# A two-layer hybrid encoder block on one core: the last third of the four mixers in another order on TensorE, VectorE and ScalarE

## The chip, the core and the metric

The kernel runs on one core of one Trainium2 chip. The metric is the device time of one execution in microseconds (us); lower is better. Beside the time of whole runs there is one profiled execution, and all rows below are of that one.

## What is computed

The block has two layers (DEPTH = 2) over 256 tokens of width 1024, in float32. Each layer normalises the input, projects it once into nine slices of 256 columns, sends the slices through four mixers of width 256 each, normalises each mixer's output by itself, joins the four, multiplies by `w_out`, scales by the gate `g1` and adds to the input. Then comes a feed-forward part: dense SwiGLU in layer 0, top-2-of-8 experts in layer 1.

```python
for l in range(DEPTH):
    mod = c_act @ w_mod[l] + b_mod[l]
    sh1, sc1, g1, sh2, sc2, g2 = jnp.split(mod, 6, axis=-1)
    h = modulate(rms_norm(x, norm_mix[l]), sh1, sc1)
    proj = h @ w_in[l]
    pa, pu, pv, px, pg, dq, dfz, di, dg = jnp.split(proj, N_IN_SLICES, axis=-1)
    ya = rms_norm(pool_mixer(pa, pool_w[l], pool_scale[l]), pool_out_norm[l])
    yb = rms_norm(sgu_mixer(pu, pv, sgu_ws[l], sgu_b[l]), sgu_out_norm[l])
    yc = rms_norm(lru_mixer(px, pg, ...), lru_out_norm[l])
    yd = hgrn_mixer(dq, dfz, di, dg, lower_bounds[l], hgrn_out_norm[l])
    y = jnp.concatenate([ya, yb, yc, yd], axis=-1) @ w_out[l]
    x = x + g1[:, None, :] * y
    h = modulate(rms_norm(x, norm_ffn[l]), sh2, sc2)
    f = swiglu(...) if l % 2 == 0 else moe_ffn(...)
    x = x + g2[:, None, :] * f
```

Mixer a is a causal pooling (a banded matrix over time, then a 64x64 product per head), b a causal spatial gating inside blocks of 128 tokens, c a gated linear recurrence, d a gated recurrence with a 64x64 state per head that is carried over chunks of 16 tokens.

## The kernel before, in words

The program is written engine by engine: TensorE, VectorE, ScalarE, GpSimd and the sync engine each have one list of instructions in a fixed order, and semaphores join them. `STEPS` names the steps that an engine marks ("mix_t" for TensorE's steps in the mixers, "mix_v" for VectorE's, "mix_a" for ScalarE's); another engine waits with `wait_ge(mix_t.sem, mix_t.at(name, l))`. VectorE and ScalarE wait for each of their own instructions to end before the next. So the order in these lists is the order of the work.

Weights come through a ring of six slots of 2 MB each; the sync engine issues their loads in the order of `chunks` and issues a load when the user of the slot's last content is done (L528). In layer 0 the order is: modulation parts sh1, sc1, the five chunks of `w_in`, then sh2, sc2, g1, g2 (two halves each), two halves of `w_out`, then the feed-forward chunks. So the first feed-forward chunk waits for the first half of g1 to be summed, the second for the second half of g1, the next two for the halves of g2.

The modulation vectors of layer 0 are summed on VectorE between the mixers' steps: `mod_part(0, n)` multiplies each 128x512 block of two chunks by a column and adds it into `mod_acc[:, n % 2]` (L1172, L1174; eight instructions to a half, n = 3 is sc2, 4 is g1, 5 is g2). TensorE then sums over the partitions: `row_sum_columns` (L687, sixteen recorded matmuls with one column) for sh and sc, `row_sum_wide` (L707, two 128x512 matmuls) for the gates. `gate` on VectorE adds the bias (L1206).

The last third of the mixers starts where TensorE ends `scores(1)` (L799: matmuls with two moving columns, for mixer d). All bank numbers below are PSUM banks.

- TensorE, in order: d's full part from the scores (L816, bank 3), d's part from the states, 60 matmuls of 64x64 by 16 columns (L823, bank 3, step "o"), b's bias and gating (L834, L839, bank 4, step "z"), in layer 0 the column sum of sc2, then the sum of squares of d over heads (L850, "ssd"), of c ("ssc", `channel_sum`, L754), a's banded product (L861, L863, "aband"), the sum of squares of b ("ssb"), a's block product (L873, "apool"), `row_sum_wide` for g1, the sum of squares of a ("ssa"). Then the output projection (L892): 32 matmuls of 128x512, each recorded as two, in four groups of eight, in the order of mixers c, d, b, a; each group waits for its mixer's normalised output ("yc1", "yd1", "yb1", "ya1"). Banks 0 to 3 hold the result.
- ScalarE: squares and square roots around these, each named sq or rt with the mixer's letter; "gu" (Gelu of pu), "pa", "pd", "ps0", "ps1" copy and scale.
- VectorE: "sf0", "sf1", b's mean and variance to "vn1", in layer 0 `mod_part(0, 4)` (both halves of g1) and the columns of sc2, "yb_raw", then for d, c, b, a in this order the reciprocal of the root (L1397 for d, 128x512; L1407 for the others, 128x256), and two scaled products to `y_t` (L1401, L1410).

After the mixers VectorE runs `gate` for g1, in layer 0 then `mod_part(0, 5)` (both halves of g2) and three subtractions that prepare the first feed-forward weights (L1436), and then the residual: for each of four banks a product (L1235) and a sum (L1237). The norm of the next part follows, and the feed-forward part begins on TensorE (L921).

Of the kernel before, what the change touches and what calls it, by code (L numbers as in the profile page):

```python
# [101 lines left out]
class Steps:  # L102
# [11 lines left out]
    def said(self, name):  # L114
# [13 lines left out]

STEPS = {
# [100 lines left out]
def hybrid_stream_block(nc, a, out):  # L230

    ctx = ExitStack()
    with ctx:
# [136 lines left out]
        def mark(ins, s, name):  # L370

            s.said(name)
# [63 lines left out]
        def mod_bank(l, n):  # L436

            return bank[7] if l == 0 and n >= 2 else bank[n] if l == 0 else bank[0]
# [233 lines left out]
        def _(eng):  # L672
# [53 lines left out]
            def mixers(l):  # L726
# [83 lines left out]
                scores(1)  # L810
                eng.wait_ge(mix_v.sem, mix_v.at("wst", l))
# [7 lines left out]
                eng.wait_ge(mix_v.sem, mix_v.at("qt", l))  # L819
                for h in range(NH):  # L820
# [6 lines left out]
                mark(ins.then_inc(mix_t.sem, 1), mix_t, "o")  # L827

                eng.wait_ge(mix_v.sem, mix_v.at("vn1", l))
                eng.wait_ge(mix_v.sem, mix_v.at("wst", l))  # L830
# [12 lines left out]
                if l == 0:  # L843
                    row_sum_columns(0, "sc2")

                eng.wait_ge(mix_a.sem, mix_a.at("sqd", l))
                eng.wait_ge(chain_v.sem, chain_v.at("s", l * CHAIN + CHAIN - 1))
                if l == 0:
                    eng.wait_ge(mod_e.sem, mod_e.at("fin", 3))
                mark(mm(bank[7][:, :], head_ones, tmp[:, 2, :], start=True, stop=True).then_inc(mix_t.sem, 1),  # L850
                     mix_t, "ssd")
                eng.wait_ge(mix_a.sem, mix_a.at("sqc", l))
                eng.wait_ge(mix_a.sem, mix_a.at("i1", l))
                channel_sum(bank[5], tmp[:, 8, :], "ssc")

                eng.wait_ge(mix_a.sem, mix_a.at("pa", l))
                eng.wait_ge(mix_v.sem, mix_v.at("sf1", l))
                eng.wait_ge(s_const, N_CONSTS)
                for g in range(NH):
                    q, i = g % 2, g // 2  # L860
                    mm(bank[6][q * HD:(q + 1) * HD, i * T:i * T + EDGE], tmp[:, 11, g * HD:(g + 1) * HD],  # L861
                       band_a[:, g, :], start=i == 0, stop=False, skip_group_check=True)
                    ins = mm(bank[6][q * HD:(q + 1) * HD, i * T + P:(i + 1) * T],  # L863
                             tmp[:, 11, G + g * HD:G + (g + 1) * HD], band_b[:, g, :],
                             start=False, stop=True, skip_group_check=True)
                mark(ins.then_inc(mix_t.sem, 1), mix_t, "aband")
                eng.wait_ge(mix_a.sem, mix_a.at("sqb", l))
                eng.wait_ge(mix_a.sem, mix_a.at("rtd", l))
                channel_sum(bank[7], tmp[:, 4, :], "ssb")
                eng.wait_ge(mix_a.sem, mix_a.at("pd", l))  # L870
                eng.wait_ge(mix_v.sem, mix_v.at("yb_raw", l))
                for i in range(CB):
                    ins = mm(bank[4][:, i * T:(i + 1) * T], blocks[:, 0, i, :], tmp[:, 6, i * T:(i + 1) * T],  # L873
                             start=True, stop=True)
                mark(ins.then_inc(mix_t.sem, 1), mix_t, "apool")
                eng.wait_ge(mix_a.sem, mix_a.at("rtb", l))
                row_sum_wide(l, 0, (bank[6], bank[7]))
                eng.wait_ge(mix_a.sem, mix_a.at("sqa", l))
                eng.wait_ge(mix_a.sem, mix_a.at("rtc", l))
                channel_sum(bank[5], tmp[:, 1, :], "ssa")  # L880
# [3 lines left out]
                for name in ("gate_d", "gu", "pa"):  # L884
                    eng.wait_ge(mix_a.sem, mix_a.at(name, l))
                eng.wait_ge(mix_v.sem, mix_v.at("od", l))
                for n, (name, g) in enumerate((("yc1", 2), ("yd1", 3), ("yb1", 1), ("ya1", 0))):
                    eng.wait_ge(mix_v.sem, mix_v.at(name, l))
                    for tt in range(TT):
                        for half in range(2):  # L890
                            for i in range(2 * g, 2 * g + 2):
                                ins = mm(bank[2 * tt + half][:, :], y_t[:, i, tt * P:(tt + 1) * P],  # L892
# [255 lines left out]
        def _(eng):  # L1148
            tt_, ts_, stt = nc.vector.tensor_tensor, nc.vector.tensor_scalar, nc.vector.scalar_tensor_tensor

            def mod_part(l, n):
# [8 lines left out]
                for half in range(2):  # L1160
# [79 lines left out]
            def mixers(l):  # L1240
                def v(ins, name):
                    done(eng, ins, mix_v, name, l)
# [146 lines left out]
                if l == 0:  # L1389
                    mod_part(0, 4)  # L1390
                    mod_columns(0, "sc2")
                eng.wait_ge(mix_t.sem, mix_t.at("z", l))
# [10 lines left out]
                for n, (name, at, rt, src, par_name) in enumerate((("c", 4, 9, 12, "lru_out"), ("b", 2, 10, 7, "sgu_out"),  # L1403
                                                              ("a", 0, 2, 3, "pool_out"))):
                    eng.wait_ge(mix_a.sem, mix_a.at(f"rt{name}", l))
                    r = t(rt)[:, 0:T]
                    v(nc.vector.reciprocal(r, r).then_inc(mix_v.sem, 1), f"rec_{name}")  # L1407
                    for i in range(CB):
                        c = slice(i * T, (i + 1) * T)
                        v(stt(out=y_t[:, at + i, :], in0=t(src)[:, c], scalar=par(par_name, l, i), in1=r,  # L1410
                              op0=ALU.mult, op1=ALU.mult).then_inc(mix_v.sem, 1), f"y{name}{i}")
# [282 lines left out]
            for l in range(DEPTH):  # L1694
# [4 lines left out]
                gate(l, 0, (bank[6], bank[7]))  # L1699
# [4 lines left out]
                residual(2 * l, [bank[n][:, :] for n in range(4)], [[(mix_t, f"wout{n}", l)] for n in range(4)])  # L1704
# [22 lines left out]
        def _(eng):  # L1727
# [27 lines left out]
            def mixers(l):  # L1755
# [64 lines left out]
                s(act(t(8), t(12), ACT.Square).then_inc(mix_a.sem, 1), "sqc")  # L1820
                eng.wait_ge(mix_v.sem, mix_v.at("vc1", l))
                for tt in range(TT):
# [5 lines left out]
                eng.wait_ge(mix_t.sem, mix_t.at("pu", l))  # L1828
                s(act(t(7), bank[1][:, :], ACT.Gelu_apprx_tanh).then_inc(mix_a.sem, 1), "gu")
                eng.wait_ge(mix_t.sem, mix_t.at("pa", l))  # L1830
                s(act(t(11), bank[2][:, :], ACT.Copy).then_inc(mix_a.sem, 1), "pa")
# [5 lines left out]
                eng.wait_ge(mix_t.sem, mix_t.at("ssc", l))  # L1837
                s(act(t(9)[:, 0:T], bank[5][:, 0:T], ACT.Sqrt, bias=eps_col[:, 0:1], scale=1.0 / G).then_inc(mix_a.sem, 1),
                  "rtc")
                eng.wait_ge(mix_t.sem, mix_t.at("aband", l))  # L1840
                s(act(t(6), bank[6][:, :], ACT.Copy).then_inc(mix_a.sem, 1), "pd")
                eng.wait_ge(mix_v.sem, mix_v.at("yb_raw", l))
                s(act(t(4), t(7), ACT.Square).then_inc(mix_a.sem, 1), "sqb")
                eng.wait_ge(mix_t.sem, mix_t.at("ssb", l))
                s(act(t(10)[:, 0:T], bank[7][:, 0:T], ACT.Sqrt, bias=eps_col[:, 0:1], scale=1.0 / G).then_inc(mix_a.sem, 1),
                  "rtb")
                eng.wait_ge(mix_t.sem, mix_t.at("apool", l))
                for i in range(CB):
                    c = slice(i * T, (i + 1) * T)
                    s(act(t(3)[:, c], bank[4][:, c], ACT.Copy, scale=par("pool_scale", l, i)).then_inc(mix_a.sem, 1),  # L1850
                      f"ps{i}")
                s(act(t(1), t(3), ACT.Square).then_inc(mix_a.sem, 1), "sqa")
                eng.wait_ge(mix_t.sem, mix_t.at("ssa", l))
                eng.wait_ge(mix_v.sem, mix_v.at("od", l))
                eng.wait_ge(mix_v.sem, mix_v.at("yd1", l))
                s(act(t(2)[:, 0:T], bank[5][:, 0:T], ACT.Sqrt, bias=eps_col[:, 0:1], scale=1.0 / G).then_inc(mix_a.sem, 1),
                  "rta")
# [229 lines left out]
```

## Time and profile before

| | |
|---|---|
| median of three runs | 1695.45 us (1695.25 to 1698.53) |
| the profiled execution | 1696.81 us |
| its span, first to last instruction | 1695.1 us |
| mean granted TensorE clock | 0.958 of full speed |
| busy: TensorE matmul, weight load | 95%, 79% |
| busy: VectorE, ScalarE | 78%, 58% |
| one of 40 slices of the page | 42.4 us |

The busy shares are averages over very different stages. The experts take the time from about 655 us to 1690 us, the dense feed-forward part that from 218 us to 470 us, and the two passes through the mixers' last third, which are what the change touches, lie from 145 us to 210 us and from 573 us to 633 us. The granted clock takes two values, 1.00 (2.4 GHz) and 0.50 (1.2 GHz); values between are stretches that hold both.

### The profile page before, as it was taken

To read this page: it belongs to the slowest core of one execution; us is meant where nothing else is said; L and a number is where in the kernel's file an instruction comes from. 1 tells how busy PE (TensorE), PEld (TensorE's weight loads), DVE (VectorE), ACT (ScalarE), POOL (GpSimd) and SP (SyncE) were. 2 spreads that over 40 slices of the span, in tenths; PEclk is the share of its full clock that TensorE was granted. 3 is DMA by queue.
4 is the path that set the end of the run, shared out by engine and by line. 5 is a ranking of instruction groups with operands and counts; after the bars stand their busy time and mean duration, and the time that the engine had idled before them with its cause. 6 is when DMAs were issued, how large, how long until landed. Compare 5 with 4: busy or idle time off the path is not lost.

```text
span 1695.1 us, 19855 instructions
## 1 busy us (share of the span) xinstructions
PE 1610.8 (95%) x8005; PEld 1332.3 (79%) x8005; DVE 1327.2 (78%) x1266; ACT 987.2 (58%) x895; POOL 38.8 (2%) x108
## 2 busy tenths in 40 slices
PE   5999889999979997999999999999999999999994
PEld 5699489999867846888888888888888888888883
DVE  5687868878666255878978978988988988988985
ACT  1442244433352325777777777777777777777772
POOL 5100000000000000000000000000000000000000
PEclk9986999999998797999999999999999999999997
DMA  9648456888832204989999999999999989999970
GB/s 354 217 149 301 166 203 248 299 309 314 295 112 100 100 25 157 367 329 368 351 329 367 349 331 362 352 334 356 357 335 350 362 332 350 360 333 351 370 269 39
DMA packets 157000, 481.07 MB, mean 284 GB/s; under 512 B 4202, under 2 KB 6422, under 8 KB 156902
## 3 DMA queue, kind: packets, MB, share of 16 engines
q1 hardware_dynamic: 154976, 475.02, 76.0%
q0 software_dynamic: 1392, 3.58, 0.7%
q8 instruction: 65, 1.06, 0.3%
q10 hardware_dynamic: 534, 1.13, 0.2%
q14 instruction: 33, 0.27, 0.0%
HBM read 478.66 MB, written 1.05 MB: 283 GB/s over the span
## 4 chain that ended last, share of the span: by engine, by line
issue 63%; PE 29%; DVE 4%; ACT 1%; DMA 1%; POOL 1%; SPq 1%; DVEq 0%; ACTq 0%; POOLq 0%
PE bank L747 4%; PE bank L892 3%; PE bank L921 3%; PE bank L922 3%; PE bank L923 3%; PE bank L799 2%; PE bank L744 2%; PE bank L936 2%; PE bank L937 2%; PE bank L938 2%; PE bank L823 1%; DMA ring<-in_w_mod_dram 1%; PE bank L687 1%; PE bank L779 1%; DVE tri L1296 1%
## 5 line engine op out<-in xcount | busy, mean ns | idle before, releaser
L1549 DVE TENSOR_TENSOR ring_low<-ring,w_high 128x2048 fp32r<-128x2048 f32 x336 | 766.8, 2292 | 128.0 <-ACT w_high L1919 121.5
L1919 ACT ACTIVATE w_high<-ring 128x2048 fp32r<-128x2048 f32 x336 | 643.8, 1919 | 243.5 <-PE bank L995 241.7
L993 PE MATMUL bank<-w_high,x_high 128*128 128x512 f32 x896 | 358.1, 400 | 1.1 <-DVE x_low L1525 1.1
L994 PE MATMUL bank<-ring_low,x_high 128*128 128x512 f32 x896 | 352.9, 394 | 0.0
L995 PE MATMUL bank<-w_high,x_low 128*128 128x512 f32 x896 | 350.0, 391 | 0.0
L995 PEld LDWEIGHTS bank<-w_high,x_low 128*128 128x128 f32 x896 | 168.4, 188 | 41.0
L993 PEld LDWEIGHTS bank<-w_high,x_high 128*128 128x128 f32 x896 | 168.5, 188 | 39.6 <-DVE ring_low L1549 1.5
L994 PEld LDWEIGHTS bank<-ring_low,x_high 128*128 128x128 f32 x896 | 167.9, 187 | 34.9
L993 PE MATMUL bank<-w_high,act_high 128*128 128x512 f32 x448 | 179.9, 402 | 3.6 <-DVE ring_low L1549 3.6
L995 PE MATMUL bank<-w_high,act_low 128*128 128x512 f32 x448 | 177.0, 395 | 0.0
L994 PE MATMUL bank<-ring_low,act_high 128*128 128x512 f32 x448 | 175.9, 393 | 0.0
L1864 ACT ACTIVATE tmp_r<-ring 128x1024 fp32r<-128x1024 f32 x84 | 88.9, 1061 | 146.4 <-PE bank L923 86.5
L1436 DVE TENSOR_TENSOR ring_low<-ring,tmp_r 128x1024 fp32r<-128x1024 f32 x84 | 102.2, 1225 | 45.5 <-ACT tmp_r L1864 43.1
L921 PE MATMUL bank<-h_high,tmp_r 128*128 128x256 f32 x448 | 128.1, 286 | 4.6 <-DVE h_low L1443 4.6
L922 PE MATMUL bank<-h_high,ring_low 128*128 128x256 f32 x448 | 127.2, 284 | 0.0
L923 PE MATMUL bank<-h_low,tmp_r 128*128 128x256 f32 x448 | 126.2, 282 | 0.0
L993 PEld LDWEIGHTS bank<-w_high,act_high 128*128 128x128 f32 x448 | 84.2, 188 | 28.9 <-DVE ring_low L1549 8.4
L995 PEld LDWEIGHTS bank<-w_high,act_low 128*128 128x128 f32 x448 | 84.0, 187 | 20.4
L994 PEld LDWEIGHTS bank<-ring_low,act_high 128*128 128x128 f32 x448 | 84.4, 188 | 18.6
L747 PE MATMUL bank<-h_t,ring 128*128 128x256 f32 x384 | 90.7, 397 | 2.3 <-POOL band_a L638 2.0
L921 PEld LDWEIGHTS bank<-h_high,tmp_r 128*128 128x128 f32 x448 | 85.8, 191 | 5.3 <-issue 5.0
L747 PEld LDWEIGHTS bank<-h_t,ring 128*128 128x128 f32 x384 | 76.2, 200 | 15.2 <-issue 2.2
(305 smaller groups left out, 1801.4 us busy)
## 6 DMA issues: line engine op xcount, KB each, us to landing
ring<-in_moe_w_dram SPq DMA_DIRECT2D x168, 2048.0 KB, 7.9
ring<-in_w_mod_dram SPq DMA_DIRECT2D x23, 2048.0 KB, 11.0
ring<-in_ffn_w_dram SPq DMA_DIRECT2D x21, 2048.0 KB, 12.0
ring<-in_w_in_dram SPq DMA_DIRECT2D x8, 2048.0 KB, 15.1
ring<-in_w_out_dram SPq DMA_DIRECT2D x4, 2048.0 KB, 14.3
ring<-in_w_mod_dram SPq DMA_DIRECT2D x2, 1024.0 KB, 15.9
ring<-in_w_in_dram SPq DMA_DIRECT2D x2, 1024.0 KB, 18.6
gate_row<-in_b_mod_dram POOLq DMA_DIRECT2D x4, 512.0 KB, 7.3
```

The source lines that it names most:

```text
L747: ins = mm(b[:, i * T:(i + 1) * T], w[:, k, off + i * P:off + (i + 1) * P], h_t[:, k, :], start=k == 0, stop=k == KB - 1)
L892: ins = mm(bank[2 * tt + half][:, :], y_t[:, i, tt * P:(tt + 1) * P], wide(("wout", l, half))[:, i, :], start=n == 0 and i == 2 * g, stop= ...
L921: mm(o, w_h[:, k, :], h_high[:, k, :], start=k == 0, stop=False)
L922: mm(o, w_l[:, k, :], h_high[:, k, :], start=False, stop=False)
L923: ins = mm(o, w_h[:, k, :], h_low[:, k, :], start=False, stop=k == KB - 1)
L993: mm(out_, x_h, w_h, start=first, stop=False)
L994: mm(out_, x_h, w_l, start=False, stop=False)
L995: return mm(out_, x_l, w_h, start=False, stop=last)
L1436: mark(tt_(quarter(ring_low, QUARTERS[m]), quarter(ring, QUARTERS[m]), quarter_high(m).bitcast(F32), ALU.subtract).then_inc(ffn_l.sem, 1), ...
L1549: tt_(moe_low(u, m // 2)[:, c], moe_slot(u, m // 2)[:, c], w_high[:, m % HIGHS, :].bitcast(F32), ALU.subtract).then_inc(low_made, 1)
L1864: mark(act(quarter_high(m), quarter(ring, QUARTERS[m]), ACT.Copy).then_inc(ffn_h.sem, 1), ffn_h, "q")
L1919: act(w_high[:, m % HIGHS, :], moe_slot(u, m // 2)[:, c], ACT.Copy).then_inc(high_made, 1)
```

## The change

The same operations are done in both layers; their order and some buffers and banks change.

- TensorE: after `scores(1)` come, in this order, in layer 0 the column sum of sc2 (now in bank 5), "ssc" (bank 0), "aband" (bank 7), d's full part, then the 60 state matmuls of d in four parts of 15 (`from_states(h)`), with "apool" (bank 6) after the first, "z" after the second, and "ssa" (bank 1) after the third. After the fourth ("o") come "ssb" (bank 2), "ssd" (bank 7) and the output projection, whose groups run in the order c, a, b, d and whose banks are 0, 1, 2 and 4.
- `row_sum_wide` for g1 moves from ahead of the projection into it, ahead of the fourth group (banks 5 and 6).
- ScalarE: "gu" and "pa" move up behind "sqc"; then "rtc", "pd", the squares and root of b's variance, "ps0", "ps1", "sqa", "rta", "sqb", "rtb", "sqd", "rtd".
- VectorE: the order of the mixers is c, a, then "yb_raw", b, d. In layer 0 the columns of sc2 come ahead of all that, the first half of g1 is summed between c and a, and the second half behind d. `gate`, `mod_part(0, 5)`, the three subtractions and the residual follow as before.

```diff
+WOUT_BANKS = (0, 1, 2, 4)
...
     "mix_v":
...
-         "cv10 cv11 cv12 xc1 qt a2 m m0 ix bb hs0 hs1 yc_raw sf0 sf1 mu vc0 vc1 rvr vn0 vn1 yb_raw rec_d "
-         "od yd0 yd1 rec_c yc0 yc1 rec_b yb0 yb1 rec_a ya0 ya1").split(),
+         "cv10 cv11 cv12 xc1 qt a2 m m0 ix bb hs0 hs1 yc_raw sf0 sf1 mu vc0 vc1 rvr vn0 vn1 rec_c "
+         "yc0 yc1 rec_a ya0 ya1 yb_raw rec_b yb0 yb1 rec_d od yd0 yd1").split(),
     "mix_a":
...
-        ("sig lna lnb lnk eb ea kh q kt xp gate_c gv0 gv1 r0 r1 i0 i1 a0 a1 th0 th1 sm gate_d sqc sv0 sv1 "
-         "rv gu pa sqd rtd rtc pd sqb rtb ps0 ps1 sqa rta").split(),
+        ("sig lna lnb lnk eb ea kh q kt xp gate_c gv0 gv1 r0 r1 i0 i1 a0 a1 th0 th1 sm gate_d sqc gu pa rtc pd "
+         "sv0 sv1 rv ps0 ps1 sqa rta sqb rtb sqd rtd").split(),
     "mix_t":
...
-        ("dfz ws di dq kt px u0 u1 u2 u3 u4 u5 u6 u7 pg pv wa wx sc0 dg pu pa sc1 o z ssd ssc aband ssb "
-         "apool ssa wout0 wout1 wout2 wout3").split(),
+        ("dfz ws di dq kt px u0 u1 u2 u3 u4 u5 u6 u7 pg pv wa wx sc0 dg pu pa sc1 ssc aband apool z ssa "
+         "o ssb ssd wout0 wout1 wout2 wout3").split(),
...
@@ TensorE, behind scores(1)
+                if l == 0:
+                    eng.wait_ge(mix_a.sem, mix_a.at("i1", l))
+                    row_sum_columns(0, "sc2")
...
+                channel_sum(bank[0], tmp[:, 8, :], "ssc")
...
+                def from_states(h):
...
+                eng.wait_ge(mix_v.sem, mix_v.at("qt", l))
+                from_states(0)
...
+                from_states(1)
...
+                from_states(2)
...
+                channel_sum(bank[1], tmp[:, 1, :], "ssa")
+                mark(from_states(3).then_inc(mix_t.sem, 1), mix_t, "o")
+                eng.wait_ge(mix_a.sem, mix_a.at("sqb", l))
+                channel_sum(bank[2], tmp[:, 4, :], "ssb")
                 eng.wait_ge(mix_a.sem, mix_a.at("sqd", l))
...
-                eng.wait_ge(mix_a.sem, mix_a.at("rtb", l))
-                row_sum_wide(l, 0, (bank[6], bank[7]))
...
-                for n, (name, g) in enumerate((("yc1", 2), ("yd1", 3), ("yb1", 1), ("ya1", 0))):
+                eng.wait_ge(mix_v.sem, mix_v.at("yb_raw", l))
+                for n, (name, g) in enumerate((("yc1", 2), ("ya1", 0), ("yb1", 1), ("yd1", 3))):
+                    if n == 3:
+                        eng.wait_ge(mix_a.sem, mix_a.at("ps1", l))
+                        if l == 0:
+                            eng.wait_ge(mod_e.sem, mod_e.at("fin", 3))
+                        row_sum_wide(l, 0, (bank[5], bank[6]))
                     eng.wait_ge(mix_v.sem, mix_v.at(name, l))
...
@@ VectorE, behind vn1
                 if l == 0:
-                    mod_part(0, 4)
                     mod_columns(0, "sc2")
...
+                scaled("c", 4, t(9)[:, 0:T], 12, "lru_out")
+                if l == 0:
+                    mod_part(0, 4, (0,))
+                scaled("a", 0, t(10)[:, T:2 * T], 8, "pool_out")
                 eng.wait_ge(mix_t.sem, mix_t.at("z", l))
                 eng.wait_ge(mix_a.sem, mix_a.at("gu", l))
                 v(tt_(t(7), t(7), bank[4][:, :], ALU.mult).then_inc(mix_v.sem, 1), "yb_raw")
+                scaled("b", 2, t(10)[:, 0:T], 7, "sgu_out")
...
+                if l == 0:
+                    mod_part(0, 4, (1,))
...
-                gate(l, 0, (bank[6], bank[7]))
+                gate(l, 0, (bank[5], bank[6]))
                 if l == 0:
                     mod_part(0, 5)
                     for m in range(HIGHS):
                         quarter_rest(m)
```

## Rows read from the trace of the kernel before

**Rows 1.** The page, section 2: the granted TensorE clock in 40 slices.

```profile
PEclk9986999999998797999999999999999999999997
```

**Rows 2.** Timeline of layer 0, VectorE: start us, us, engine, line.

```profile
185.95 1.42 DVE L1206 TENSOR_TENSOR gate_row<-bank,gate_row 128x512 f32<-128x512 f32 x2
...
193.96 5.48 DVE L1174 SCALAR_TENSOR_TENSOR mod_acc<-ring,c_act,mod_acc 128x512 f32<-128x512 f32 x7
...
199.47 3.50 DVE L1436 TENSOR_TENSOR ring_low<-ring,tmp_r 128x1024 fp32r<-128x1024 f32 x3
...
202.99 0.69 DVE L1235 TENSOR_TENSOR h_t<-bank,gate_row 128x512 f32<-128x512 f32 x1
...
208.94 0.69 DVE L1237 TENSOR_TENSOR x<-x,h_t 128x512 f32<-128x512 f32 x1
```

**Rows 3.** Timeline of layer 0, TensorE: scores, states, sums, projection.

```profile
134.80 10.61 PE L799 MATMUL bank<-head_sel,tri 128*128 128x2 f32 x64
...
146.38 1.97 PE L816 MATMUL bank<-v_wide,tmp 128*64 128x128 f32 x16 [0.97 <-DVE v_wide L1372]
...
148.28 11.78 PE L823 MATMUL bank<-tmp,state 64*64 64x16 f32 x120
...
163.90 3.58 PE L687 MATMUL bank<-consts,mod_acc 128*128 128x1 f32 x16
...
180.40 27.70 PE L892 MATMUL bank<-ring,xn 128*128 128x512 f32 x64 [0.89 <-DVE xn L1410]
```

**Rows 4.** Timeline of layer 0, the single operations that change places.

```profile
169.93 1.91 PE L754 MATMUL bank<-tmp,consts 128*128 128x256 f32 x4
...
170.22 1.28 ACT L1835 ACT_TABLE_LOAD   x1 [9.46 <-PE bank L850]
...
172.31 3.35 DVE L1397 RECIPROCAL tmp<-tmp 128x512 f32<-128x512 f32 x1 [3.63 <-ACT tmp L1835]
...
173.92 0.63 ACT L1843 ACTIVATE tmp<-tmp 128x512 f32<-128x512 f32 x1
...
174.60 1.13 PE L754 MATMUL bank<-tmp,consts 128*128 128x256 f32 x4 [1.41 <-ACT tmp L1843]
...
175.83 0.47 ACT L1845 ACTIVATE tmp<-bank,eps_col 128x256 f32<-128x256 f32 x1 [1.28 <-PE bank L754]
...
176.43 1.91 PE L707 MATMUL bank<-mod_acc,consts 128*128 128x512 f32 x4
176.69 0.98 ACT L1850 ACTIVATE tmp<-bank,params 128x256 f32<-128x256 f32 x2 [0.39 <-PE bank L873]
...
177.46 1.75 DVE L1407 RECIPROCAL tmp<-tmp 128x256 f32<-128x256 f32 x1
...
179.25 1.01 DVE L1410 SCALAR_TENSOR_TENSOR xn<-tmp,params 128x256 f32<-128x256 f32 x2
```

**Rows 5.** Windows of TensorE: length, busy (matmul records), granted clock, DMA share, GB/s.

```profile
100.20:103.90 3.70, 3.70 (x35) 1.00 0.95 359
104.00:110.00 6.00, 6.00 (x30) 0.50 0.30 112
110.30:114.00 3.70, 3.70 (x10) 0.50 0.00 0
```

**Rows 6.** Timeline of layer 1: TensorE and VectorE.

```profile
563.45 9.32 PE L799 MATMUL bank<-head_sel,tri 128*128 128x2 f32 x64
...
603.60 27.70 PE L892 MATMUL bank<-ring,xn 128*128 128x512 f32 x64 [0.86 <-DVE xn L1410]
...
632.14 0.69 DVE L1237 TENSOR_TENSOR x<-x,h_t 128x512 f32<-128x512 f32 x1
```

**Rows 7.** Windows of all engines: PE, PEld, DVE, ACT, POOL, clock, DMA.

```profile
152.00:156.00 4.00, 4.00 (x44) 4.00 (x44) 3.82 (x6) 1.19 (x2) 0.00 (x0) 0.50 1.05 386
...
218.00:470.00 252.00, 248.12 (x1748) 232.35 (x1748) 189.42 (x215) 101.75 (x104) 0.00 (x0) 0.99 0.76 275
```

**Rows 8.** Timeline of layer 0, the sync engine's loads of feed-forward weights.

```profile
157.87 41.96 SPq L528 DMA_DIRECT2D ring<-in_ffn_w_dram  x4
```

More of the change, by code:

```diff
@@ L436, in mod_bank @@
         def mod_bank(l, n):
-            return bank[7] if l == 0 and n >= 2 else bank[n] if l == 0 else bank[0]
+            return bank[(0, 1, 7, 5)[n]] if l == 0 else bank[0]
         def slot(n):
@@ L854, in mixers @@
[L854 to L874, printed above, removed]
@@ L875, in mixers @@
-                mark(ins.then_inc(mix_t.sem, 1), mix_t, "apool")
-                eng.wait_ge(mix_a.sem, mix_a.at("rtb", l))
-                row_sum_wide(l, 0, (bank[6], bank[7]))
-                eng.wait_ge(mix_a.sem, mix_a.at("sqa", l))
-                eng.wait_ge(mix_a.sem, mix_a.at("rtc", l))
-                channel_sum(bank[5], tmp[:, 1, :], "ssa")
                 for half in range(2):
                     arrived(eng, ("wout", l, half))
-                for name in ("gate_d", "gu", "pa"):
+                for name in ("rtc", "rta", "rtb"):
@@ L891, in mixers @@
                             for i in range(2 * g, 2 * g + 2):
-                                ins = mm(bank[2 * tt + half][:, :], y_t[:, i, tt * P:(tt + 1) * P],
+                                ins = mm(bank[WOUT_BANKS[2 * tt + half]][:, :], y_t[:, i, tt * P:(tt + 1) * P],
                                          wide(("wout", l, half))[:, i, :], start=n == 0 and i == 2 * g,
@@ L1159, in mod_part @@
                     eng.wait_ge(gate_t.sem, gate_t.at("sum", 2 * (l - 1) + n))
-                for half in range(2):
+                for half in halves:
                     key = ("mod", l, MOD_PARTS[n], half)
@@ L1402, in mixers @@
                           op0=ALU.mult, op1=ALU.mult).then_inc(mix_v.sem, 1), f"yd{i}")
[L1403 to L1411, printed above, removed]
+                if l == 0:
+                    mod_part(0, 4, (1,))
             def mod_step(n, step):
@@ L1703, in _ @@
                         quarter_rest(m)
-                residual(2 * l, [bank[n][:, :] for n in range(4)], [[(mix_t, f"wout{n}", l)] for n in range(4)])
+                residual(2 * l, [bank[n][:, :] for n in WOUT_BANKS], [[(mix_t, f"wout{n}", l)] for n in range(4)])
                 norm_x(2 * l + 1)
@@ L1827, in mixers @@
                   "rv")
[L1828 to L1831, printed above, removed]
+                eng.wait_ge(mix_t.sem, mix_t.at("apool", l))
+                for i in range(CB):
+                    c = slice(i * T, (i + 1) * T)
+                    s(act(t(8)[:, c], bank[6][:, c], ACT.Copy, scale=par("pool_scale", l, i)).then_inc(mix_a.sem, 1),
+                      f"ps{i}")
+                s(act(t(1), t(8), ACT.Square).then_inc(mix_a.sem, 1), "sqa")
+                eng.wait_ge(mix_t.sem, mix_t.at("ssa", l))
+                s(act(t(10)[:, T:2 * T], bank[1][:, 0:T], ACT.Sqrt, bias=eps_col[:, 0:1], scale=1.0 / G).then_inc(mix_a.sem, 1),
+                  "rta")
+                eng.wait_ge(mix_v.sem, mix_v.at("yb_raw", l))
+                s(act(t(4), t(7), ACT.Square).then_inc(mix_a.sem, 1), "sqb")
+                eng.wait_ge(mix_t.sem, mix_t.at("ssb", l))
+                s(act(t(10)[:, 0:T], bank[2][:, 0:T], ACT.Sqrt, bias=eps_col[:, 0:1], scale=1.0 / G).then_inc(mix_a.sem, 1),
+                  "rtb")
                 eng.wait_ge(mix_t.sem, mix_t.at("o", l))
@@ L1836, in mixers @@
                   "rtd")
[L1837 to L1857, printed above, removed]
             def quarter_first(m):
@@ L2044, in _ @@
                 if l == 0:
[L2045 removed]
+                    eng.wait_ge(mix_v.sem, mix_v.at("yd1", l))
                     for m in range(HIGHS):
```

52 lines of the change are left out of this document (38 added, 14 removed).

## The prediction

> **What bounds the kernel now.** I read the page's clock line first, then timelines of both mixer tails with all engines, then windows for the clock, last the sync engine's loads. The clock line shows full speed nearly everywhere with dips where the mixers run [rows 1]. In the tail of layer 0 TensorE is the path: scores, states, norm sums, then the projection without a break from 180.40 for 27.70 us, eight matmuls in 27.70/4 = 6.93 us [rows 3]. Behind the last mixer's output VectorE has a row of its own that is as long: gate at 185.95 (1.42), g2's two halves from there to 193.96 + 5.48 = 199.44 (12.04, so 6.0 a half), three subtractions to 202.97, and at 202.99 the residual [rows 2]. From the start of the gate to the residual that is 17.04 us with no idle time. TensorE's first result bank is done at 180.40 + 20.8 + 1.7 = 202.9. So both engines arrive together, with no slack on either. The residual ends at 209.63 [rows 2]. In layer 1 g2 is summed elsewhere, VectorE waits for TensorE, and the residual ends at 632.83 [rows 6].
>
> **The pieces, at both clocks.** TensorE's clock falls in the scores although it is never idle there: 35 records in 3.70 us at 1.00, 30 in 6.00 at 0.50 [rows 5]. So loads of weights also take twice as long at half clock. A norm sum (two 128x256 matmuls) takes 1.85 at half clock before the next matmul starts (1.91 to its end) and 0.87 at full, being 1.13 with its drain [rows 4]; until ScalarE starts I take 2.1 and 1.25. apool has the same shape. The full part takes 1.9 at half, aband with 1088 columns for 1024 takes 2.0. The states take 11.78 at half clock, 2.93 a quarter [rows 3, 7], and by the ratio of the scores 1.47 at full. From the states' end (160.06) to the sc2 sum (163.90) z takes 3.9 at half, 2.0 at full; the sc2 sum 3.5 to the next matmul [rows 3]. ScalarE: square 0.65, root 0.47, the two scalings 0.98. A mixer's three VectorE steps take 1.75 + 1.01 = 2.8 with the gap; d's end needs 3.35 first [rows 4]. yb_raw reads and writes 128x512 once, as a residual product does: 0.7 [rows 2].
>
> **Edit 1, the reordering up to the projection.** Two schedules bound it. In H the clock stays at 0.50 until the projection. In F it comes back once ssc, aband and the full part (5.75 us of dense matmuls) are through, holds over the states, and is lost again where TensorE runs dry before ssb.
>
> Layer 0, H, from the scores' end at 145.4: sc2 sum 148.95, ssc 150.8, aband 152.8, full part 154.7, states 157.6, apool 159.3, states 162.3, z 166.2, states 169.1, ssa 171.0, rta 171.7. Now a chain over three engines: a on VectorE 174.6, yb_raw 175.3, sqb 176.05, ssb for ScalarE 178.2, rtb and sqd 179.35, ssd 181.2. The projection starts at 181.2, against 180.40. F is equal to 154.7, then 156.2, 157.0, 158.5, 160.5, 162.0, 162.85, rta 163.5. Here VectorE is late: g1's first half runs from 159.4 to 165.4. So a 168.2, yb_raw 168.9, sqb 169.7, ssb (half clock again, as TensorE was idle for 5 us) 171.8, rtb and sqd 172.95, ssd 174.85: the projection starts at 174.85.
>
> Layer 1 begins at 563.45 + 9.32 = 572.8 [rows 6]. H by the same steps: full part 578.6, rta 595.6, sqb 600.0, ssd 605.15. F: full part 578.6, ssa 586.75, rta 587.35, sqb 591.7, ssd 596.85, against 603.60 before. To F I add 1.0 us for small gaps at changes of matmul form, which the sums of lengths leave out; layer 0 hides it behind VectorE.
>
> The new waits sit on ScalarE: behind sqb wait rtb, sqd, rtd, all of them needed. b's variance now stands behind rtc and pd, ends at about 155 and gives vn1 at 156.2, while z starts after 158.5: hidden by 2 us. The function table load ahead of rtd, 1.28 us [rows 4], leaves the path; new loads ahead of gu and rtc are hidden by the scores and by the same 2 us.
>
> **Edit 2, the projection.** Groups c, a, b are ready at its start or 3 us after, d some 6 us after ssd (0.7 + 3.35 + 0.7 + 1.01); d is needed 20.8 us on. All hidden. `row_sum_wide` was in a gap of the old norm chain; it now adds its two 128x512 matmuls, 1.73 us, to both projections. At the start the clock is low in both schedules. After scores(0) dense work ran at 0.50 for 4 us [rows 5]; ssd is 1.85 of them, the other 2.1 cost half, 1.1 us (bounds 0 and 1.8).
>
> **Edit 3, what waits for the gate.** This is the large term. `gate` needs `row_sum_wide`, which now stands behind three groups, and g2's sums, the subtractions and the residual stand behind `gate` on VectorE. g1's second half ends near 187 (F) or 194 (H) and VectorE then idles. With the projection starting at S: three groups 20.8, clock 1.1, wide sum 1.73 and 0.17 to VectorE, then the 17.04 us above, then the residual of 4 x 1.45 = 5.8. The residual ends at S + 46.6. Before it ended at S + 29.2. Layer 0: F 221.5, that is +11.9; H 227.8, +18.2. In layer 1 VectorE has no g2 sum and TensorE sets the end: S + 1.1 + 1.73 + the 29.2 of before, so F 597.85 + 32.0 = 629.9, -3.0 against 632.83 (gaps included), and H 637.2, +4.3.
>
> What makes this certain is that TensorE's matmuls run in the order of its list. The Trainium skill says so in "TensorE: Matmul & The Clock Gate", section "Step-by-step: what each phase is for": only weight loads are pulled ahead of running matmuls, the matmuls stay in program order. The trace agrees, each group of rows 3 starts after the one ahead of it; could the wide sum pass the first groups, it would run when g1 is done and layer 0 would lose some 9 us less.
>
> **Loads.** SP's queue is moved too. The first feed-forward chunk was issued at 157.87 when g1's first half was summed [rows 8]; it goes at about 165.4, the second at about 187 to 194, g2's two behind the late sums at about 206 to 219. ScalarE needs the second for its third preparation, ahead of the residual at 215; it has over 15 us. The others are needed in the ninth step or later of a part that begins after 229. Nothing, but if the second came 15 us late it would add directly.
>
> **The sum.** F: +11.9 - 3.0 = +8.9. H: +18.2 + 4.3 = +22.5. F in one layer alone: +16.2 or +15.3. All behind moves along one for one: in the dense part TensorE is busy 248.12 of 252 us at 0.99 clock [rows 7], so its start sets its end. I take F, since the one stretch of rows 5 where dense work followed scores came back in 4 us and here 5.75 are dense. The profiled execution took 1696.81, its span 1695.1 and 1.7 outside; the median is 1695.45. F gives 1705.7 for the profiled and 1704.4 for the median.
>
> **Rivals.** (1) H, or H in one layer: the dense stretch before the states does not bring the clock back, or the states lose it again. For it: the scores lost it while TensorE was busy, and it stays at half all through the states [rows 7]. 1711 to 1718. (2) The clock stays up to the end of the projection. By the skill's same page, section "What's actually happening", the clock follows how busy the engine has been lately; TensorE is never idle from the scores to the end of the states, and read so it would be full early and stay. Worked out from rows: ssb and ssd at full save 1.85, the projection 1.1, in each layer: +8.9 - 5.9 = +3, 1698.5. Rows 5 speak against busy alone being enough. (3) The other side, not slower: the lost time is absorbed. If the dense part waited for weights, a later start would cost nothing from the point where the ring is 12 us behind; layer 0 would be neutral and layer 1's -3.0 would be left, 1692.5. Rows 7 speak against it: DMA at 0.76 and TensorE idle under 4 us. (4) The norm tail's chain in layer 0 is longer than I took (VectorE later than 165.4): up to +3 on F.
>
> **Chances.** F 0.50, with (4) 0.10 inside; one layer H 0.22, both H 0.13, (2) 0.10, (3) 0.02, the rest 0.03 near no change. The range leaves out (3) and most of both H: 1698 to 1716. A change of 0.2%, 3.4 us, is about what a measurement of this kernel tells from none. Faster 0.03, same 0.07, slower 0.90.
>
> **What would show it.** In the profile after: in layer 0 an idle stretch of VectorE of over 8 us that ends at `gate` on TensorE's wide sum; the residual starting 17 us behind it and long after the last projection matmul; TensorE idle for some 20 us between projection and next norm. In layer 1 a projection of 29.5 us or more with the wide sum inside and no such gap. Clock windows between 155 and 165 tell F (1.00) from H (0.50). I am wrong if `gate` runs before the projection's third group ends, or if the dense part is shorter than before.

## The result and the profile after

The changed kernel takes 1709.8 us (median of four runs, 1709.19 to 1710.39) against 1696.09 us before: a ratio of 1.0078, 95% interval 1.0061 to 1.0096. The prediction was 1704.4 with a range of 1698 to 1716 and 0.90 on slower. The profiled execution has a span of 1707.4 us against 1695.1.

To compare the two traces I count from the end of `scores(1)`, where the changed part begins, to the start of the output projection and from there to the end of the residual. F and H are the two schedules of the prediction: in F the full clock comes back for the states, in H it stays at half up to the projection.

| us | before | after | F | H |
|---|---|---|---|---|
| layer 0: scores' end to projection | 35.0 | 31.5 | 29.5 | 35.8 |
| layer 0: projection to residual's end | 29.2 | 47.4 | 46.6 | 46.6 |
| layer 0, sum | 64.2 | 78.9 | 76.1 | 82.4 |
| layer 1: scores' end to projection | 30.8 | 28.0 | 25.1 | 32.4 |
| layer 1: projection to residual's end | 29.2 | 31.9 | 32.0 | 32.0 |
| layer 1, sum | 60.1 | 59.9 | 57.1 | 64.4 |

So the changed parts are 14.7 us longer in layer 0 and 0.1 us shorter in layer 1. These are the parts of one profile; further passes follow with the experiments. The spans differ by only 12.3 because this execution came to the end of layer 0's scores 3.7 us sooner, and lost 1.5 us elsewhere; none of that code is touched (the last section tells why such differences occur).

The timeline of VectorE in layer 0, after. The rows answer to [rows 2]; the bracket is the idle time ahead of a row and what ended it.

```profile
179.96 5.48 DVE L1186 SCALAR_TENSOR_TENSOR mod_acc<-ring,c_act,mod_acc 128x512 f32<-128x512 f32 x7
...
197.91 1.42 DVE L1218 TENSOR_TENSOR gate_row<-bank,gate_row 128x512 f32<-128x512 f32 x2 [12.47 <-PE bank L710]
...
199.89 5.48 DVE L1186 SCALAR_TENSOR_TENSOR mod_acc<-ring,c_act,mod_acc 128x512 f32<-128x512 f32 x7
...
205.92 5.48 DVE L1186 SCALAR_TENSOR_TENSOR mod_acc<-ring,c_act,mod_acc 128x512 f32<-128x512 f32 x7
211.43 3.50 DVE L1455 TENSOR_TENSOR ring_low<-ring,tmp_r 128x1024 fp32r<-128x1024 f32 x3
...
214.85 0.68 DVE L1247 TENSOR_TENSOR h_t<-bank,gate_row 128x512 f32<-128x512 f32 x1
...
219.92 0.69 DVE L1249 TENSOR_TENSOR x<-x,h_t 128x512 f32<-128x512 f32 x1
```

g1's second half is summed at 185.44, and then VectorE stands idle for 12.47 us until the wide sum (now L710) is there. Gate, g2's sum, the subtractions and the residual follow without a break, from 197.91 to 220.61. The timeline of TensorE, after, answers to [rows 3]:

```profile
132.07 9.65 PE L802 MATMUL bank<-head_sel,tri 128*128 128x2 f32 x64
...
153.37 1.92 PE L848 MATMUL bank<-tmp,state 64*64 64x16 f32 x30
...
157.65 3.38 PE L848 MATMUL bank<-tmp,state 64*64 64x16 f32 x30
...
168.00 2.07 PE L757 MATMUL bank<-tmp,consts 128*128 128x256 f32 x4 [1.66 <-ACT tmp L1866]
...
171.33 2.07 PE L886 MATMUL bank<-tmp,consts 128*128 128x512 f32 x2 [1.25 <-ACT tmp L1871]
...
173.19 22.87 PE L904 MATMUL bank<-ring,xn 128*128 128x512 f32 x48
...
195.90 1.88 PE L710 MATMUL bank<-mod_acc,consts 128*128 128x512 f32 x4
...
197.61 7.03 PE L904 MATMUL bank<-ring,xn 128*128 128x512 f32 x16
...
221.65 3.68 PE L719 MATMUL bank<-consts,xn 128*128 128x128 f32 x16 [17.00 <-DVE xn L1226]
```

The wide sum stands at 195.90, behind three groups of the projection. The projection is done at 204.64, which is 62.9 us behind the scores' end (62.7 before), and then TensorE waits 17.00 us for a norm that VectorE brings late. The chain of work that ended last, in order of time, runs over the same points:

```profile
179.75 16.31 PE bank L904 x38
196.06 1.73 PE bank L710 x4
197.91 0.70 DVE gate_row L1218
...
211.43 3.50 DVE ring_low L1455 x3
...
220.84 0.76 DVE xn L1226
```

In layer 1 VectorE also waits for the wide sum, 17.48 us, but has no g2 to sum behind it, and the residual keeps up with TensorE. Timelines of both engines, answering to [rows 6]:

```profile
612.16 21.84 PE L904 MATMUL bank<-ring,xn 128*128 128x512 f32 x48
...
633.84 1.88 PE L710 MATMUL bank<-mod_acc,consts 128*128 128x512 f32 x4
...
635.56 7.03 PE L904 MATMUL bank<-ring,xn 128*128 128x512 f32 x16
635.86 1.42 DVE L1218 TENSOR_TENSOR gate_row<-bank,gate_row 128x512 f32<-128x512 f32 x2 [17.48 <-PE bank L710]
...
643.42 0.69 DVE L1249 TENSOR_TENSOR x<-x,h_t 128x512 f32<-128x512 f32 x1
```

The clock in layer 0, windows of all engines, after (the clock is the third number from the right), answering to [rows 7]:

```profile
144.00:149.50 5.50, 5.50 (x33) 4.67 (x34) 0.25 (x1) 2.05 (x3) 0.00 (x0) 0.50 1.05 387
151.00:156.00 5.00, 5.00 (x65) 4.56 (x64) 4.36 (x9) 1.79 (x4) 0.00 (x0) 1.00 1.05 387
157.50:162.00 4.50, 4.50 (x36) 4.13 (x34) 3.89 (x6) 0.00 (x0) 0.00 (x0) 0.50 0.85 309
...
173.00:177.00 4.00, 4.00 (x6) 1.69 (x5) 3.22 (x3) 0.69 (x1) 0.00 (x0) 0.50 0.00 2
178.00:195.00 17.00, 17.00 (x41) 7.47 (x40) 7.09 (x11) 3.06 (x3) 0.00 (x0) 1.00 0.36 124
```

It was back at 150, as F has it, and gone again at 157, ahead of the third quarter of the states, while TensorE was busy without a gap. The second quarter took 1.92 us, the third 3.38. In the kernel before the clock stood at half from the scores through the states, but it was back at 172.3, 8 us ahead of the projection, and that projection ran at full clock from its start. Windows of TensorE, before (the clock is again the third number from the right):

```profile
171.50:172.00 0.50, 0.50 (x3) 0.50 1.03 381
172.50:173.00 0.50, 0.50 (x12) 1.00 1.05 389
```

### The profile page after: what moved, and what is told of

Its sections match the earlier page's. It is cut to its first block, busy times and chain, and to the rows that moved or that the text cites. A ratio compares the mean times of both kernels' runs of the same rounds, so it can differ in the third digit from the quotient of the medians.

```text
span 1707.4 us, 19844 instructions
## 1 busy us (share of the span) xinstructions
PE 1609.9 (94%) x8005; PEld 1327.9 (78%) x8005; DVE 1328.4 (78%) x1266; ACT 985.0 (58%) x893; POOL 38.8 (2%) x108
## 4 chain that ended last, share of the span: by engine, by line
issue 62%; PE 30%; DVE 4%; DMA 1%; ACT 1%; POOL 0%; SPq 0%; DVEq 0%; ACTq 0%; POOLq 0%
PE bank L750 4%; PE bank L933 3%; PE bank L934 3%; PE bank L935 3%; PE bank L904 3%; PE bank L802 2%; PE bank L747 2%; PE bank L948 2%; PE bank L949 2%; PE bank L950 1%; DMA ring<-in_w_mod_dram 1%; PE bank L690 1%; PE bank L848 1%; PE bank L757 1%; PE bank L782 1%
## 5 line engine op out<-in xcount | busy, mean ns | idle before, releaser
L1455 DVE TENSOR_TENSOR ring_low<-ring,tmp_r 128x1024 fp32r<-128x1024 f32 x84 | 102.2, 1225 | 46.6 <-ACT tmp_r L1881 44.2
```

Source lines behind the costliest of these rows:

```text
L1455: mark(tt_(quarter(ring_low, QUARTERS[m]), quarter(ring, QUARTERS[m]), quarter_high(m).bitcast(F32), ALU.subtract).then_inc(ffn_l.sem, 1), ...
```

## The experiments

Four kernels (g2's sum ahead of gate, the wide sum one group earlier, the new order in layer 1 alone, the wide sum in the gaps) ran on one chip with 32 runs of the kernel before (median 1696.64), the other four on another chip with 11 (median 1695.91). The ratios are to the kernel before on the same chip. They are estimates with an interval and not quotients of two medians, from which they differ by up to 0.2%, so both are given where it matters. "The two parts" are, for one profiled execution, the times of the table above.

**g2's sum ahead of gate.** Edit of the changed kernel, on VectorE in layer 0:

```diff
-                gate(l, 0, (bank[5], bank[6]))
                 if l == 0:
                     mod_part(0, 5)
+                gate(l, 0, (bank[5], bank[6]))
+                if l == 0:
                     for m in range(HIGHS):
                         quarter_rest(m)
```

> The changed kernel with one edit on VectorE in layer 0: the sum of g2 (12.0 us) goes ahead of gate instead of behind it. Theory: the loss is the chain wide sum, gate, g2, subtractions, residual. The 12.5 us that VectorE idled ahead of gate then hold g2's sum; gate, the subtractions and the residual follow the wide sum at once, so the residual starts some 12 us earlier (202.9 instead of 214.85 on the changed kernel's clock) and the kernel takes 1709.8 - 12 = 1698. Rival, the norm chain or the wide sum inside the projection is the loss: no more than 2 us come back. Rival, the dense part's weights come late: no change.

Measured: 1702.88 us, ratio 1.0031 (1.0017 to 1.0045). In the profile the two parts of layer 0 are 31.5 + 35.3 = 66.7 us, 12.1 less than in the changed kernel. Timeline of VectorE of this kernel:

```profile
191.55 5.48 DVE L1186 SCALAR_TENSOR_TENSOR mod_acc<-ring,c_act,mod_acc 128x512 f32<-128x512 f32 x7
197.35 1.42 DVE L1218 TENSOR_TENSOR gate_row<-bank,gate_row 128x512 f32<-128x512 f32 x2 [0.32 <-PE bank L710]
198.80 3.50 DVE L1455 TENSOR_TENSOR ring_low<-ring,tmp_r 128x1024 fp32r<-128x1024 f32 x3
202.22 0.68 DVE L1247 TENSOR_TENSOR h_t<-bank,gate_row 128x512 f32<-128x512 f32 x1
```

The idle 12.47 us ahead of gate are 0.32 now. The trace shows the 12 us. Whole runs show 7 by the medians (1709.8 to 1702.88) and 8 by the ratios (1.0078 to 1.0031 is 0.47%), where 12 and 1698 were expected. This profile lost 5.5 us against the changed kernel's in a stretch of layer 1 that no edit touches (the last section). That most of the other runs lost it there too is not shown. The theory holds for the chain; the size in whole runs came out smaller than expected.

**The wide sum one group earlier.** Edit on TensorE:

```diff
-                    if n == 3:
+                    if n == 2:
                         eng.wait_ge(mix_a.sem, mix_a.at("ps1", l))
```

> The changed kernel with one edit on TensorE: the wide sum of g1 stands ahead of the third group of the projection instead of the fourth. Theory: g1 is summed at 185.4, the third group would begin at about 189, so the wide sum ends 6.9 us (one group of eight matmuls) earlier in layer 0, and gate, g2's sum and the residual with it; layer 1 keeps its time, since there TensorE sets the end and the projection is as long. 1709.8 - 6.9 = 1703. Rival, VectorE's order alone matters and not the wide sum's place: no change. Rival, the length of the projection is the loss: no change.

Measured: 1708.49 us, ratio 1.0050 (1.0033 to 1.0067), single runs from 1703.54 to 1710.3. In layer 0 the part behind the projection's start is 39.6 us, 7.8 less than 47.4: one group (6.93) and 0.9 because this projection lost less to half clock. Timelines of VectorE and TensorE:

```profile
194.59 1.88 PE L710 MATMUL bank<-mod_acc,consts 128*128 128x512 f32 x4
```

```profile
196.60 1.42 DVE L1218 TENSOR_TENSOR gate_row<-bank,gate_row 128x512 f32<-128x512 f32 x2 [4.67 <-PE bank L710]
```

gate starts 16.9 us behind the projection's start (179.69) instead of 24.7, and the residual's end moves with it. The place of the wide sum in TensorE's list counts, not VectorE's order alone. In this execution the projection itself began 2.8 us later than in the changed kernel's profile, counted from the scores' end. The whole did not reach the forecast of 1703: it gained 1.3 us by the medians and 4.7 by the ratios, whose intervals just overlap. So this experiment stands on its trace, not on its whole runs.

**The new order in one layer alone.** Both kernels hold both orders of the three engines' `mixers` and of the step lists and take one for each layer:

```diff
+            def mixers(l):
+                (mixers_old, mixers_new)[l](l)      # layer1_only; the other: (mixers_new, mixers_old)
```

> Layer 0 in the old order, layer 1 in the new one. The changed kernel's trace has the loss in layer 0 (+14.8 us from the end of the scores to the end of the residual) and -0.1 in layer 1. Theory: 1696 within 1 us, the same as before. My F schedule said -3.0 for layer 1 and H +4.3; 1693 or 1700 would say that layer 1's share in the one profile was chance. Rival, the loss lies evenly in both layers: 1703.

> Layer 0 in the new order, layer 1 in the old one. Theory: all of the loss is here: 64.2 us from the end of the scores to the end of the residual become 77 to 79, layer 1 stays at 60.1, the kernel is 13 to 15 us slower than before. Rival, the two layers share the loss: 7 us slower.

Measured: new in layer 1 alone 1699.39 us, ratio 1.0003 (0.9987 to 1.0020); new in layer 0 alone 1707.95 us, ratio 1.0079 (1.0057 to 1.0101). Parts of layer 0 in the latter 31.5 + 47.3 = 78.8, of layer 1 in the former 28.1 + 33.0 = 61.1. The loss is layer 0's. By its ratio layer 1's share is 0.5 us, with an interval from -2.2 to +3.4; by the medians it is 2.8, which misses the forecast of 1696 within 1 us, and layer 0's is 12.0 (13.4 by the ratio) where 13 to 15 were forecast, with 78.8 us for its parts, inside the 77 to 79. The five profiled passes of layer 1 in the new order that leave its wide sum in the projection took 59.9, 61.1, 61.1, 62.7 and 62.7 us (the changed kernel, g2 first, layer 1 alone, the wide sum one group earlier, the changed kernel again), the two in the old order 60.1 and 59.8. So layer 1 costs 0 to 3 us, and the -0.1 of the first profile was the favourable end.

**g1 earlier and the wide sum in the gaps.** The longest edits of the core:

```diff
                       f"vc{tt}")
+                if l == 0:
+                    mod_part(0, 4, (0,))
...
                 if l == 0:
-                    mod_part(0, 4, (0,))
+                    mod_part(0, 4, (1,))
                 scaled("a", 0, t(10)[:, T:2 * T], 8, "pool_out")
...
                 mark(from_states(3).then_inc(mix_t.sem, 1), mix_t, "o")
+                wide_half(l, 0, (bank[5], bank[6]), 0)
                 eng.wait_ge(mix_a.sem, mix_a.at("sqb", l))
                 channel_sum(bank[2], tmp[:, 4, :], "ssb")
+                wide_half(l, 0, (bank[5], bank[6]), 1)
...
-                        row_sum_wide(l, 0, (bank[5], bank[6]))
```

> The changed kernel with g1 summed earlier and the wide sum off the projection: on VectorE g1's first half goes into the 7 us of idle time behind vc1, its second half between c and a; on TensorE the two matmuls of the wide sum go singly into the gaps ahead of ssb and ahead of ssd, in both layers. Theory: in layer 0 gate runs directly behind d's output, g2 is summed under the projection, and TensorE sets the end again: residual's end 15 to 17 us earlier; in layer 1 the projection is 1.7 us shorter and ssd at most 0.4 us later. 1709.8 - 17 - 1.5 = 1691 to 1692, faster than both. Rival, layer 0's loss is not the gate's chain: over 1700. Clock: the gaps are filled with dense matmuls, so it could come back a little sooner in the projection, up to 1 us a layer.

Measured: 1693.25 us, ratio 0.9968 (0.9953 to 0.9982): faster than both, some 1.5 us short of the forecast. Layer 0: 33.9 + 29.1 = 63.0, layer 1: 30.5 + 29.2 = 59.7. The part behind the projection is back at the 29.2 of before in both layers. But the projection begins 2.4 us later than in the changed kernel in layer 0 and 2.5 in layer 1, where 0.4 was expected. Timeline of TensorE of this kernel:

```profile
172.89 2.07 PE L719 MATMUL bank<-mod_acc,consts 128*128 128x512 f32 x2
...
174.76 1.94 PE L767 MATMUL bank<-tmp,consts 128*128 128x256 f32 x4
...
176.48 1.92 PE L719 MATMUL bank<-mod_acc,consts 128*128 128x512 f32 x2
...
178.19 1.40 PE L901 MATMUL bank<-tmp,consts 128*128 128x512 f32 x2
```

The first matmul of the wide sum (172.89) holds ssb up by 0.2 us (sqb had ended at 174.56), the second (176.48) ssd by 0.3 (sqd had ended at 177.89): together the 0.4 that was expected. The other 2 us are the clock, which in this execution had gone down again at 158.5, ahead of z, and in layer 1 3.5 us after it came back. Passes of the changed kernel with the same clock took 34.3 and 30.9 to the projection (the kernel again, below), so beside those nothing was lost in front of it. The clock was back at 179.0, 0.4 us ahead of the projection, which ran at full clock from its start, as the expectation had allowed for; and 62.7 us of layer 1 became 59.7.

**Dense work between the states.** Six extra matmuls in each layer, whose results nobody reads:

```diff
+                def fill(b):
+                    mm(b[:, :], h_t[:, 2, 0:P], h_t[:, 0:2, :].rearrange("p k t -> p (k t)"), start=True, stop=True)
...
                 from_states(0)
+                fill(bank[2])
```

> The changed kernel with six added 128x512 matmuls into unused banks in each layer: one behind each of the first three quarters of the states, two in the gap ahead of ssb, one ahead of ssd. Their results are not used. It tests the step of my F schedule that failed, that the clock, once back, holds over the states. Theory: the states themselves lose it, dense work between them keeps it; each filler costs 0.87 us and only three of them are not in gaps, the quarters take 1.8 instead of 3.3, ssb and ssd 0.9 instead of 1.85, and the projection starts at full clock: 2 to 4 us faster in each layer, 1703 when the changed kernel has 1709. Rival, the clock goes down again whatever runs: the fillers cost 1.7 each, 5 to 7 us slower a layer.

Measured: 1710.69 us, ratio 1.0080 (1.0059 to 1.0100), against 1.0088 for the changed kernel on the same chip: no difference. Windows of all engines of this kernel, layer 0:

```profile
145.00:150.00 5.00, 5.00 (x35) 4.17 (x35) 0.00 (x0) 2.86 (x5) 0.00 (x0) 0.50 1.05 385
150.00:155.00 5.00, 5.00 (x58) 3.93 (x55) 3.76 (x8) 1.61 (x5) 0.00 (x0) 1.00 1.05 387
155.00:160.00 5.00, 5.00 (x59) 3.92 (x58) 4.75 (x8) 0.77 (x2) 0.00 (x0) 1.00 0.87 317
160.00:165.00 5.00, 5.00 (x22) 3.12 (x21) 1.17 (x2) 0.00 (x0) 0.00 (x0) 0.52 0.50 168
165.00:170.00 5.00, 5.00 (x33) 4.11 (x33) 3.41 (x4) 1.10 (x2) 0.00 (x0) 0.50 0.67 253
170.00:175.00 5.00, 4.78 (x9) 2.36 (x7) 0.51 (x1) 1.05 (x3) 0.00 (x0) 0.61 0.00 0
175.00:180.00 5.00, 4.93 (x12) 2.30 (x13) 4.89 (x4) 0.71 (x2) 0.00 (x0) 1.00 0.01 2
```

The full clock lasted from 150 to 160.3, 10 us instead of 7, and was lost in the third quarter all the same, so the next three fillers ran at half clock. It was back at 173.9, ahead of ssd, and the projection started at full clock, as forecast: its first three groups took 20.6 us (22.7 in the changed kernel's first profile, 21.6 in its second). But the projection began 34.7 us behind the scores' end in layer 0 and 31.3 in layer 1, no sooner than in the later of the changed kernel's passes. In whole runs neither side's forecast came true: what the clock gives, the fillers eat.

**The changed kernel again.** 

> The changed kernel again, as the reference for the other three on the same chip. Expected 1705 to 1710: single runs of one kernel lie up to 8 us apart here, since the clock of TensorE comes back at other moments in stretches that the change does not touch.

Measured: 1712.2 us, ratio 1.0088 (1.0071 to 1.0105), above the expected 1705 to 1710. The profiled execution has a span of 1717.8, with 34.3 + 46.3 = 80.6 in layer 0 and 30.9 + 31.7 = 62.7 in layer 1.

**One chain less before the projection.** On top of the kernel with the gaps:

```diff
-                scaled("a", 0, t(10)[:, T:2 * T], 8, "pool_out")
                 v(tt_(t(7), t(7), bank[4][:, :], ALU.mult).then_inc(mix_v.sem, 1), "yb_raw")
+                scaled("a", 0, t(10)[:, T:2 * T], 8, "pool_out")
...
                 channel_sum(bank[1], tmp[:, 1, :], "ssa")
+                eng.wait_ge(mix_a.sem, mix_a.at("sqb", l))
+                channel_sum(bank[2], tmp[:, 4, :], "ssb")
                 mark(from_states(3).then_inc(mix_t.sem, 1), mix_t, "o")
...
+                    if n == 1:
...
+                        wide_half(l, 0, (bank[5], bank[6]), 1)
...
+                if l == 0:
+                    mod_part(0, 5)
                 gate(l, 0, (bank[5], bank[6]))
                 if l == 0:
-                    mod_part(0, 5)
```

> From the kernel with the wide sum in the gaps: on VectorE yb_raw goes ahead of a's three steps, on ScalarE sqb ahead of rta, on TensorE ssb ahead of the last quarter of the states, so that only sqd and ssd stand between the states and the projection; the wide sum's first matmul ahead of ssd, its second behind the projection's first group; in layer 0 the sum of g2 ahead of gate. Theory: TensorE's idle 2.9 us between the states and the projection go down to under 1, of which the wide sum's half takes all and adds 1: the projection starts 1 to 2 us earlier than in the kernel with the gaps, the end of the residual comes 1 to 2 us earlier in each layer, 1690 to 1692. Rival, another wait takes its place (g1's second half delays yb_raw in layer 0): gain in layer 1 alone, 1692.

Measured: 1688.52 us, ratio 0.9939 (0.9920 to 0.9959): 7 us faster than the kernel before by the medians and 10 by the ratio, and 24 faster than the changed one on the same chip. Layer 0: 30.2 + 31.0 = 61.2, layer 1: 26.4 + 31.0 = 57.4. Timelines of TensorE (the view ends at 176, inside the last row) and VectorE:

```profile
167.60 2.07 PE L719 MATMUL bank<-mod_acc,consts 128*128 128x512 f32 x2
...
169.47 1.92 PE L899 MATMUL bank<-tmp,consts 128*128 128x512 f32 x2
...
171.17 5.02 PE L915 MATMUL bank<-ring,xn 128*128 128x512 f32 x9
```

```profile
189.49 1.42 DVE L1229 TENSOR_TENSOR gate_row<-bank,gate_row 128x512 f32<-128x512 f32 x2
190.94 3.50 DVE L1466 TENSOR_TENSOR ring_low<-ring,tmp_r 128x1024 fp32r<-128x1024 f32 x3
195.54 0.69 DVE L1258 TENSOR_TENSOR h_t<-bank,gate_row 128x512 f32<-128x512 f32 x1 [1.11 <-PE bank L915]
```

TensorE has no gap between the last states and the projection, and VectorE is ready 1.11 us ahead of TensorE's first result bank. The projection starts 3.7 and 4.1 us sooner than with the gaps alone, more than the 1 to 2 expected; for an estimated 2 to 3 us of it the clock of this execution is the reason (full for 7 us in both layers, in the other for 3.5): passes of the changed kernel differ by 2.8 and 2.9 with the same two lengths. Against the changed kernel's first profile, where it also lasted 7 us, the projection starts 1.3 and 1.6 us sooner. From there to the residual's end it takes 31.0 where the kernel with the gaps took 29.1: the first group runs partly at half clock (7.9 us up to the wide sum instead of 6.9) and one matmul of the wide sum, 0.9 us, is inside.

## Why the prediction was right, step by step

**Edit 3, the gate's chain, was the cause.** The wait, its place and its releaser were as written: VectorE idle for 12.47 us (over 8 said), ended by the wide sum; from gate to the residual 16.94 us (17.04); from the projection's start to the residual's end 47.4 (46.6); TensorE idle for 17.00 us ahead of the norm (some 20). The g2 experiment takes the idle time away and 12.1 us go; the experiment with the wide sum one group earlier takes one group's time and 7.8 go; the kernel with the wide sum ahead of the projection takes all of it. With the old order in layer 0 and the new one in layer 1 the ratio is 1.0003. That TensorE keeps its matmuls in the order of the list, which the Trainium skill states in "TensorE: Matmul & The Clock Gate", section "Step-by-step: what each phase is for", agrees: in each kernel the wide sum ran exactly behind the group it was written behind, though g1 had been summed 10.5 us before in the changed one.

**Edit 2** was right in kind: the wide sum adds 1.7 us to both projections. The half clock at the start was mis-sized: 1.1 us forecast, 1.9 in layer 0 (22.7 us from 173.19 to 195.90 where three groups at full clock take 20.8) and 0.9 in layer 1; over the other passes without fillers whose projection holds the whole wide sum it was 0.7 to 2.0.

**Edit 1** had the step that failed: "holds over the states, and is lost again where TensorE runs dry before ssb". The clock came back in the dense stretch or the first states behind it in every one of the 16 passes profiled in the new order, at 8 to 10 us behind the scores' end in layer 0 and 3 to 6 in layer 1, so H came true nowhere. But it was lost 3 to 7 us later (10 with the fillers), in the states' second or third quarter or in z, with TensorE busy. That is 2.0 us on layer 0's way to the projection (31.5 against F's 29.5) and 2.9 on layer 1's (28.0 against 25.1, gaps included). Both layers came out between F and H. The start of the projection falls on two values: 31.5 in three passes and 34.3 in two in layer 0, 28.0 to 28.1 in three and 30.9 in two in layer 1. The later ones, nearer to H, are those where the full clock lasted 3 us and not 7. The old order has no such spread in its four passes (35.0 twice, 30.8 and 30.5); it runs the states at half clock each time. One price of F was wrong too: a quarter of the states, priced at 1.47 us at full clock and 2.93 at half, took 1.85 and 3.31 up to the next matmul. Three quarters lie on layer 1's path; this is 1.1 us, which the 1.0 us put in for small gaps covers.

**The sum.** F gave +8.9; measured +13.7 in the medians and, in the one profile, +14.7 - 0.1 in the changed parts. The difference to F of 5.7 in the profile is 2.0 + 0.8 in layer 0 and 2.9 in layer 1, nearly all of it clock: an estimate from this profile's rows has layer 1 lose 3.9 us to half clock (z 3.4 where it takes 2.1 at full clock, the third quarter 3.3 for 1.9, ssa 2.0 for 0.9) and get 1.5 back, because the dense stretch ended 4.3 us behind the scores' end where F has 5.8. So the forecast came out near because the gate's chain, its large term, was right; F was low by 5 us in the medians, on the side of H. That is the first rival in part of its size. **The others:** the clock never stayed up to the end of the projection (2). Nothing was absorbed (3): from the start of the dense part to the scores of layer 1 it took 314.3 us before and 314.5 after. VectorE was not the late one ahead of the projection (4) in layer 0: g1's first half ended at 161.57, 2.1 us ahead of a's first step. **Loads:** ScalarE waited 11.91 us for the second feed-forward chunk and had it at 193.41, 23 us ahead of its next work, as costed at nothing.

## What to carry to other kernels

When a short operation is moved in one engine's fixed order, price what stands behind its reader on the other engine, not the operation: here 1.7 us of matmul, moved back by 23 us against the scores' end, made a 17 us row of VectorE start 15.7 us later, in the one layer that had that row. Put long work that doesn't need the late result ahead of the wait. Where a clock comes and goes at other moments in each execution, compare parts of the trace counted from a common point, and the medians of many runs, not two spans.

## What the runs showed of the hardware that was not expected

TensorE's clock goes down while the engine is busy: in all ten profiles in the scores, and in the new order again in the states or in z, as at 157 in layer 0 of the changed kernel between windows with no idle time. The Trainium skill has the clock follow how busy the engine has been lately ("TensorE: Matmul & The Clock Gate", section "What's actually happening"); busy in the sense of this trace's busy column does not decide it, since in both 151 to 156 and 157.5 to 162 that column is full.

The moment at which it comes back in one and the same code differs between executions. Between the two scores of layer 1, code that no edit touches, it was at half for 7 us in the profile of before and for 13.5 in that of the kernel with g2 first, and from scores(0) to the end of scores(1) they took 40.5 and 45.7 us. Over the ten profiles this stretch took 40.2 to 40.6 us in six, with about 7 us at half, 44.0 and 44.4 in two, with about 10, and 45.7 in two, with about 13.5. Windows of before, and then of that kernel:

```profile
537.50:544.50 7.00, 7.00 (x27) 6.34 (x27) 2.86 (x11) 2.78 (x7) 0.00 (x0) 0.51 0.02 8
```

```profile
535.50:549.00 13.50, 13.50 (x51) 12.31 (x52) 5.19 (x18) 5.12 (x14) 0.00 (x0) 0.51 0.16 64
```

So a difference of 5 us between two profiles need not come from an edit; the parts counted from the end of the scores show what does. Whether this also makes the scatter of single runs (1694.56 to 1703.55 for the kernel before) is not shown: their mean clocks, 0.952 to 0.959, do not sort them by time. What brings the clock back sooner in one execution than in the next stays open.
